# First mixer of a 10-stage network: another order for the first inverse steps, and one level-0 block on VectorE

## What is computed

```python
def rwkv7_step(S, inp):
    r_t, w_t, k_t, v_t, kk_t, a_t = inp
    sa = jnp.einsum("bhvk,bhk->bhv", S, -kk_t)
    S = (S * w_t[:, :, None, :]
         + jnp.einsum("bhv,bhk->bhvk", sa, kk_t * a_t)
         + jnp.einsum("bhv,bhk->bhvk", v_t, k_t))
    y = jnp.einsum("bhvk,bhk->bhv", S, r_t)
    return S, y
```

## Time and profile before

| | us |
|---|---|
| three runs | 3398.59, 3401.41, 3403.41 |
| median | 3401.41 |
| profiled execution, its own time | 3401.35 |
| its span in the profile | 3399.5 |

### The profile page before, as it was taken

One profiled execution on the slowest core, in us unless ns is written; L12 is line 12 of the kernel. 1 busy time (PEld: TensorE's weight loads), 2 busy tenths in 40 slices (PEclk: granted clock), 3 DMA queues, 4 the chain that ended last, 5 costly groups with the idle time before them and its releaser, 6 DMA issues.

```text
span 3399.5 us, 44329 instructions
## 1 busy us (share of the span) xinstructions
PE 3335.5 (98%) x18735; PEld 2694.9 (79%) x18735; DVE 1975.5 (58%) x2897; ACT 1365.8 (40%) x2088; POOL 30.4 (1%) x68
## 2 busy tenths in 40 slices
PE   8999999999999999999999999999999999999998
PEld 6888878788888888886688888757888887588887
DVE  5554597675546653435564435576765465677644
ACT  4332367443324332326543322364543243654433
POOL 0000003000000000000000000000000000000000
PEclk9999999999999999999999999999999999999999
DMA  5444340244443432231022234111333242023231
GB/s 181 148 143 148 125 137 3 94 131 149 149 143 118 161 112 94 89 100 37 32 93 99 94 99 148 64 37 50 99 99 99 93 143 69 13 81 99 94 101 60
DMA packets 93078, 342.32 MB, mean 101 GB/s; under 512 B 10320, under 2 KB 10832, under 8 KB 92368
## 3 DMA queue, kind: packets, MB, share of 16 engines
q1 hardware_dynamic: 92880, 339.48, 30.5%
HBM read 337.34 MB, written 2.10 MB: 100 GB/s over the span
## 4 chain that ended last, share of the span: by engine, by line
PE 89%; DVE 6%; ACT 4%; issue 1%; DMA 0%; POOL 0%; SPq 0%; DVEq 0%; ACTq 0%; POOLq 0%
PE ps L810 21%; PE ps L812 21%; PE ps L811 21%; PE ps L912 2%; PE ps L913 2%; PE ps L916 2%; PE ps L959 1%; PE ps L961 1%; PE ps L960 1%; PE ps L1346 1%; PE ps L935 1%; PE ps L936 1%; PE ps L937 1%; ACT WK L2178 1%; PE ps L1499 1%; DVE SPL L2287 1%
## 5 line engine op out<-in xcount | busy, mean ns | idle before, releaser
L2287 DVE TENSOR_TENSOR SPL<-RAW,SPH 128x1024 fp32r<-128x1024 f32 x522 | 635.9, 1223 | 865.2 <-ACT SPH L1592 864.6
L1592 ACT ACTIVATE SPH<-RAW 128x1024 fp32r<-128x1024 f32 x522 | 548.1, 1056 | 977.1 <-PE ps L812 862.9
L810 PE MATMUL ps<-HH,SPH 128*128 128x512 f32 x2312 | 910.7, 394 | 9.6 <-DVE SPL L2287 7.7
L812 PE MATMUL ps<-HH,SPL 128*128 128x512 f32 x2312 | 900.5, 389 | 0.0
L811 PE MATMUL ps<-HL,SPH 128*128 128x512 f32 x2312 | 900.5, 389 | 0.0
L810 PEld LDWEIGHTS ps<-HH,SPH 128*128 128x128 f32 x2312 | 434.3, 188 | 111.8 <-issue 11.1
L811 PEld LDWEIGHTS ps<-HL,SPH 128*128 128x128 f32 x2312 | 434.4, 188 | 92.6 <-issue 3.6
L812 PEld LDWEIGHTS ps<-HH,SPL 128*128 128x128 f32 x2312 | 434.4, 188 | 91.0
L810 PE MATMUL ps<-AH,SPH 128*128 128x512 f32 x996 | 389.0, 391 | 0.7 <-DVE AH L2639 0.7
L812 PE MATMUL ps<-AH,SPL 128*128 128x512 f32 x996 | 387.5, 389 | 0.0
L811 PE MATMUL ps<-AL,SPH 128*128 128x512 f32 x924 | 359.5, 389 | 0.0
(11 more groups left out here) (562 smaller groups left out, 4300.1 us busy)
## 6 DMA issues: line engine op xcount, KB each, us to landing
RAW<-in_ws SPq DMA_DIRECT2D x522, 512.0 KB, 3.3
RAW<-in_wa SPq DMA_DIRECT2D x96, 512.0 KB, 3.5
WK<-in_sm SPq DMA_DIRECT2D x2, 2784.0 KB, 9.6
WK<-in_cst SPq DMA_DIRECT2D x2, 1664.0 KB, 7.4
X<-in_x SPq DMA_DIRECT2D x8, 256.0 KB, 8.2
out<-X SPq DMA_DIRECT2D x8, 256.0 KB, 2.3
WK<-in_sm SPq DMA_DIRECT2D x1, 768.0 KB, 4.9
PCT<-in_pc SPq DMA_DIRECT2D x1, 349.0 KB, 2.9
```

Of the source, the lines that this page charges most:

```text
L810: e.matmul(out, wh, rhs[0], start=start, stop=False)
L812: mm = e.matmul(out, wl, rhs[0], start=False, stop=stop)
L1592: e.activation(SPH[:, q:q + 1024], RAW[:, r:r + 1024], ACT.Copy).then_inc(hi_ready.did(("hi", n)))
L2287: e.tensor_tensor(SPL[:, q:q + 1024], RAW[:, r:r + 1024], SPH[:, q:q + 1024].bitcast(F32), ALU.subtract).then_inc(lo_ready.did(("lo", n)))
```

## The change

The four lists get another order up to about the 30th entry, and one entry is new. On PE, `lt` of chunks 1 and 0 come first, then `vt` (into banks 4 to 7), then `nm 0 1` and `nm 1 1`; `lt 2` and `lt 3` stand between the steps of chunks 0 and 1, both `gates` go behind the first levels, and `tr 0` takes the place that `vt` had. On DVE a new kind of entry `w0 0` does level 0 of chunk 0 (three operations) right behind `LB 0`; POOL keeps the other three chunks and does chunk 1 before its memsets. `conv 0` and `conv 1`, which stood among the first entries of DVE, go behind the second level. On ACT, `ltm 1` and `ltm 0` and the four `vtc` go ahead of `gelu 0` and `gelu 1`; `kt 0`, `bt 0` go back. The entries behind these keep their order; in particular `iu 0`, `nmc 3 1`, `nmc 1 3`, `gm2 0`, `wt 3 1`, `w 3 1` on DVE and `tanh 0`, `bonb` (4), `gelu 2`, `gelu 3`, `p2 0` on ACT.

```diff
 MIX0_TENSOR
-("01", "lt", 1), ("23", "lt", 0), ("45", "lt", 3), ("67", "lt", 2), ("23", "tr", 0),
...
+("01", "lt", 1), ("23", "lt", 0), ("4567", "vt"), ("0", "nm", 0, 1), ("1", "nm", 1, 1),
...
 MIX0_VECTOR
-("LB", 1), ("LB", 0), ("conv", 1), ("LB", 2), ("w", 0, 0), ("LB", 3), ("w", 1, 0), ("conv", 0),
...
+("LB", 1), ("LB", 0), ("w0", 0), ("w", 0, 0), ("w", 1, 0), ("nmc", 0, 1), ("nmc", 1, 1),
...
 MIX0_SCALAR
-("xc", 0), ("xc", 1), ("gelu", 0), ("gelu", 1), ("ltm", 0), ("ltm", 1), ("kt", 0), ("bt", 0),
...
+("xc", 0), ("xc", 1), ("ltm", 1), ("ltm", 0), ("vtc", 0), ("vtc", 1), ("vtc", 2), ("vtc", 3),
...
 MIX0_POOL
-("t64",), ("w0", 1), ("w0", 0), ("tt0",), ("w0", 2), ("w0", 3),
+("w0", 1), ("t64",), ("tt0",), ("w0", 2), ("w0", 3),
...
 vector_program, inverse
+                    elif what == "w0":
+                        v, wt = inv["LB"][c].rearrange("p (u x) -> p u x", u=8), u8(Wc[:, 256:512])
+                        w.wait_ge(("LB", c), ("bon", 3))
+                        e.tensor_tensor(wt, v[:, :, 0:32], v[:, :, 32:64], ALU.add).then_inc(dve_done.did(("w0a", c)))
+                        w.wait_ge(("w0a", c))
+                        e.tensor_tensor(wt, wt, b8(LV[:, 320:352]), ALU.mult).then_inc(dve_done.did(("w0b", c)))
+                        w.wait_ge(("w0b", c))
+                        e.tensor_tensor(wt, wt, b8(inv["DIAG"]), ALU.add).then_inc(dve_done.did(("wt", c, 0)))
```

More of the change, by code:

```diff
@@ L196 @@
 BONUS_SUMS_AT, BONUS_AT = {12: 0, 15: 1, 18: 2, 21: 3}, {13: 0, 16: 1, 19: 2}
-MIX0_TENSOR = [("01", "lt", 1), ("23", "lt", 0), ("45", "lt", 3), ("67", "lt", 2), ("23", "tr", 0),
[3 rows of a table removed]
+MIX0_TENSOR = [("01", "lt", 1), ("23", "lt", 0), ("4567", "vt"), ("0", "nm", 0, 1), ("1", "nm", 1, 1),
[3 rows of a table added]
                ("1", "nm", 1, 3), ("5", "dd", 3, 1), ("0", "nm", 0, 3), ("6", "dd", 1, 3), ("7", "nm", 3, 2),
@@ L220 @@
                ("6", "fvar", 3), ("2", "out", 3)]
-MIX0_VECTOR = [("LB", 1), ("LB", 0), ("conv", 1), ("LB", 2), ("w", 0, 0), ("LB", 3), ("w", 1, 0), ("conv", 0),
-               ("nmc", 1, 1), ("nmc", 0, 1), ("MKm", 0, 1, 0), ("MKm", 0, 1, 1), ("w", 2, 0), ("wt", 1, 1),
[3 rows of a table removed]
+MIX0_VECTOR = [("LB", 1), ("LB", 0), ("w0", 0), ("w", 0, 0), ("w", 1, 0), ("nmc", 0, 1), ("nmc", 1, 1),
[3 rows of a table added]
+               ("MKm", 0, 0, 0), ("MKm", 0, 0, 1), ("conv", 1), ("iu", 0), ("nmc", 3, 1), ("nmc", 1, 3), ("gm2", 0), ("wt", 3, 1), ("w", 3, 1),
                ("nmc", 0, 3), ("wt", 1, 3), ("iu", 1), ("nmc", 3, 2), ("w", 1, 3), ("wt", 0, 3), ("hy", 0),
@@ L238 @@
                ("fy", 3), ("fn", 3), ("ylo", 3)]
[L239 to L242, removed]
+MIX0_SCALAR = [("xc", 0), ("xc", 1), ("ltm", 1), ("ltm", 0), ("vtc", 0), ("vtc", 1), ("vtc", 2), ("vtc", 3),
+               ("ltm", 2), ("ltm", 3), ("gelu", 0), ("gelu", 1), ("tanh", 0), ("bonb", 2), ("bonb", 3), ("bonb", 1), ("bonb", 0), ("gelu", 2),
+               ("gelu", 3), ("p2", 0), ("tanh", 1), ("sq", 0), ("p2", 1), ("xc", 2), ("sq", 1), ("kt", 0),
+               ("bt", 0), ("xc", 3), ("nmc", 0, 5), ("nmc", 1, 5), ("w5", 0), ("w5", 1),
                ("nmc", 0, 6), ("tanh", 2), ("r0", 0), ("nmc", 3, 5), ("tanh", 3), ("nmc", 1, 6), ("p2", 2),
@@ L249 @@
                ("fq", 3), ("frs", 3, False), ("yhi", 3)]
-MIX0_POOL = [("t64",), ("w0", 1), ("w0", 0), ("tt0",), ("w0", 2), ("w0", 3), ("wideT", 1), ("wideT", 0), ("wide", 0),
+MIX0_POOL = [("w0", 1), ("t64",), ("tt0",), ("w0", 2), ("w0", 3), ("wideT", 1), ("wideT", 0), ("wide", 0),
              ("wide", 1), ("wideT", 3), ("wide", 3), ("wideT", 2), ("wide", 2)]
@@ L2645, in mix0 @@
                         lru(what, *x)
-                    elif what in ("LB", "nmc", "w", "wt"):
+                    elif what in ("LB", "nmc", "w", "wt", "w0"):
                         inverse(what, *x)
```

## The result

The changed kernel takes 3413.1 us (median of 6 runs, 3409.08 to 3417.89), the kernel before 3400.82 (6 runs): a ratio of 1.0035, 95% interval 1.0023 to 1.0046. So it is 12.3 us slower. The profiled execution is the slowest of the six, 3417.89 us with a span of 3415.8, 16.3 above the span of before; what follows is an account of this execution. Of the mean granted clock, which the record lists for every run, the six have 0.991 to 0.993, while the runs of the kernel before that stand beside the experiments have 0.995 or 0.996 in all that took less than 3400.2 us and 0.992 to 0.994 in all that took more than 3402.

The account below looks back on a forecast made before the run. PE bounds the kernel, by its idle time and clock: 3401.35 + 2.85 (waits, less 0.9 for tr 0 in vt's place) + 4.6 (clock fall) = 3408.8 us; range 3402.0 to 3412.5.

Parts of the forecast that it names:

- The start: First lt to nm 0 1: nm 0 1 starts at 526.9 after a wait of 1.3 where there were 3.66.
- The waits of the levels: PE waits 1.0 ahead of dd 2 1, 0.7 gates 0, 3.1 gates 1, 3.8 us nm 3 2.
- The chain over ACT: tanh 0 to the end of p2 0, 10.0 us; delays gm2 0, so PE waits 3.8 us ahead of nm 3 2.
- The clock term: Clock falls by nm 3 2; five narrow steps there at 0.92 more each, +4.6 us, bounds 0 and 6.2.
- 2.85 of waits: Sum without the clock: PE 3.75 us later at nm 3 2, less 0.9 for tr 0 in vt's place; +2.85 us.
- C: Rival: clock falls earlier, at the first narrow pair or gates 1; 2 to 4 us more, say 3412; chance 0.13.
- B: Rival: same waits, but the clock holds at nm 3 2 or its fall is over by then; 3404.2; chance 0.22.
- E: Rival: the chain over gm2 0 doesn't decide, gm2 0 by 547; whole 6.7 us won, 3394.7; chance 0.04.

Follow-up runs that it names:

- act_early: The changed kernel with the four bonb and gelu 2, gelu 3 ahead of tanh 0 on ACT; 3412.33 us, ratio 1.0029.
- fill_after_2: fill_after with 8 more transposes in tr 0 (16) and 12 ahead of nm 0 6; 3407.95 us, ratio 1.0022.
- fill_after: The changed kernel with added transposes in three waits: 8 ahead of dd 2 1, 24 ahead of gates 1, 24 ahead of nm 3 2; 3408.15 us, ratio 1.0022.
- level_on_pool: The changed kernel with level 0 of chunk 0 back on POOL, behind w0 1 and ahead of the memsets; 3414.94 us, ratio 1.0039.
- level_alone: The kernel before with only level 0 of chunk 0 moved to DVE, w 0 0 and w 1 0 right behind it; 3408.34 us, ratio 1.0026.
- dense_a: Another order of the four lists up to r0B 0, wide steps between narrow ones, same work, w0 0 on DVE; 3417.55 us, ratio 1.0043.

## Why the prediction was wrong

The direction was right (slower, the likelier side), the size was not: 3408.8 forecast, range to 3412.5, 3413.1 measured. For the profiled execution the miss is 9.1 us, and it is that small by luck: the clock cost 13.5 more than its term (step 3), and half speed hid 4.9 of the waits (step 4). By its steps:

1. **The start.** Right. Forecast: `nm 0 1` 5.0 us behind the first `lt`, after a wait of 1.3; measured 528.17 - 522.60 = 5.6 and 1.70. `w0 0` took 0.42 + 0.83 + 0.82 and the steps between, 2.15 us; I had 1.8. The factor beside POOL was sized too low: 2 on the second and third operation, not 1.3. The clock stayed at 1.00 there in this execution, as forecast; in act_early and fill_after_2, with the same start, it fell there for 3.4 us.
2. **The waits of the levels.** Right in size at full clock: `dd 2 1` 1.0 forecast and 0.79 measured in act_early, `gates 0` 0.7 and 0.50, `gates 1` 3.1 and 3.08; `nm 3 2` 3.8 and, in fill_after, 2.84 filled and 0.71 left. In the changed kernel itself they were 0.80, none, 1.25 and 1.23, because PE came later to them at half speed. The chain over ACT was as walked: from `tanh 0` to the end of `p2 0` 556.52 + 0.63 - 547.26 = 9.9 us (10.0 forecast).
3. **The clock term.** This is the step that failed. It said that the clock falls "by `nm 3 2`" and that five narrow steps follow at 0.92 each, +4.6, at most 6.2. But the clock fell at `dd 2 1`, 17 us ahead of `nm 3 2`, behind 0.80 us, one of the two shortest waits I had walked. Slow were twelve narrow steps by 552.20 - 550.48 - 0.92 = 0.8, two `gates` by 0.95, and `RB 0` and `MK 1 0` by 0.8: 9.6 + 1.9 + 1.6 = 13.1 us. The second slow stretch, which I did not have at all, adds 10.2 us at half speed, up to 5.
4. **The sum with these terms.** 2.85 of waits, less 9.9 - (1.70 + 0.80 + 1.25 + 1.23) = 4.9 that half speed hid, plus 13.1 and 5: 16.0 us, against 16.3 between the spans. Of these 0.7 stand already ahead of the first `lt`; from there to the wait of a later stage (1575.44 here, 1559.55 before) the changed kernel takes 1052.84 - 1037.66 = 15.2 us more. In the page this is 15.9 us more busy time and 0.4 us more idle time.
5. **The rivals.** C (the clock falls earlier, 3412) is nearest to what happened, and I gave it 0.13; the place was neither of the two it named. Its 3410 to 3414 holds the 3413.1, but not for its reason: its price of 2 to 4 us was again too low, and the waits that half speed hid made up for it. B's waits were about right: in fill_after it is 7.7 us more than before from the first `lt` (521.14) to that wait of the later stage (1566.53), and 2.6 without the half of its 10.2 us at half speed, against 2.85. E did not occur: `gm2 0` ran at 557.18.

Why I went wrong can be said: my own walk put 3.1 us of waiting ahead of `gates 1`, more than the two waits that had lowered the clock in the kernel before, and I still let it fall only at the next wait. And I had it come back with the next wide steps, as behind `MK` and `gates` in rows 2. But both `gates` of the changed kernel ran at half speed, and it stayed down; in act_early, fill_after_2 and level_on_pool, in turn, it was back after 3.4 us among `nm`, `lt` and `dd`. So wide work alone does not decide the return. Nor do rows 7 speak for B: in the changed kernel the clock falls at the same wait, between wide matmuls (0.51 in the window behind it), as it does in ten of the fourteen profiles:

```profile
1575.44 0.99 PE L1346 MATMUL ps<-WK 128*128 128x384 f32 x2 [2.28 <-DVE WK L2688]
```

```profile
1576.10:1579.50 3.40, 3.40 (x13) 2.44 (x11) 2.90 (x8) 2.87 (x6) 0.00 (x0) 0.51 0.41 140
```

What stays open: what decides at a given wait. The wait of 0.8 ahead of `dd 2 1` lowered the clock in the profile of the changed kernel, and left it in those of act_early and level_on_pool, with the same PE instructions ahead of it; that it held there in fill_after does not by itself show that the fill held it. At `gates 1` it does more: with the wait of 3.08 open the clock fell in both of these, and with the wait filled it held in fill_after and fill_after_2. Nor does a fall need a wait. In the kernel before, in a later stage, the clock fell at about 2865.5 amid 64 narrow matmuls, with PE busy throughout:

```profile
2862.28 4.19 PE L1475 MATMUL ps<-WK 64*128 64x32 f32 x64
```

```profile
2864.00:2866.00 2.00, 2.00 (x36) 2.00 (x35) 1.36 (x2) 0.00 (x0) 0.00 (x0) 0.86 0.16 25
```

The changed kernel's runs spread over 9 us, level_alone's over 24. I can say that work put into the waits kept the clock up in most of these runs, not when it falls.

## What to carry to other kernels

Price a wait of TensorE by the clock too, and not by its length alone: in a run of narrow matmuls 30.7 us at half clock began behind a wait of 0.80 us, and the two `gates` that ran in it did not end it. Look at the page first: if PE's busy time grew at the same count of matmuls, as here by 15.9 us, the loss is likely the clock, as it was here, and the table of waits explains little. Before moving wide steps (`vt`, `gates`) out of a narrow stretch, ask which waits they stood next to; and time such a kernel often, since its runs can fall into groups.

## What the runs showed of the hardware

- A state that lasts. From 541 to 563 the kernel before goes through the same stretch, without a named wait, at full speed (a pair of `nm` 2.03, a single one 1.10); in the changed kernel the same narrow steps at 0.50, and the two `gates` among them, did not bring the clock back for 30.7 us. In act_early it came back at 570.1, while `MK 1 0` ran; in the changed kernel at 572.6, 1.4 us behind it.
- The Trainium skill, "TensorE: Matmul & The Clock Gate", section "Why this matters for your kernels", names a long idle gap of PE as what lowers the clock. Here it fell behind 0.80 us, and at 2865.5 in the kernel before behind no wait at all, so the measurement goes further than the page; the 3.08 us in act_early agree with it.
- VectorE beside GpSimd: 0.83 and 0.82 for an operation on 128x256 that takes 0.42 alone, while POOL ran its own level 0. In dense_a, where POOL's level 0 began only at 527.57, the same two operations took 0.42 each (the two rows below). The Trainium skill, "GPSIMD Engine Reference", section "8. Key points", has the two contend; the trace agrees, with a factor of 2.

```profile
525.74 0.42 DVE L2585 TENSOR_TENSOR SCR<-SCR,WK 128x256 f32<-128x256 f32 x1
526.20 0.42 DVE L2587 TENSOR_TENSOR SCR<-SCR,WK 128x256 f32<-128x256 f32 x1
```
